# A decoder layer on one core: one ones-product for the FFN norm's squares, and one transpose for both halves of the FFN convolution's columns

## The chip, the core and the metric

The kernel runs on one core of one Trainium2 chip. The core has five engines that run side by side, each with its own queue of instructions: PE (TensorE, matrix products into the PSUM banks), ACT (ScalarE), DVE (VectorE), POOL (GpSimd) and SP, which here only issues DMAs. They wait for each other on counting semaphores. The metric is the device time of one execution in microseconds (us); lower is better.

## The reference

One inference step of a hybrid decoder layer on 512 prompt tokens and 8 x 8 sample tokens, which share all weights. Attention and mLSTM heads give `h`; the change touches only what follows `h`:

```python
def causal_dwconv(x, buf, w):
    width, s = w.shape[0], x.shape[1]
    xx = jnp.concatenate([buf.astype(x.dtype), x], axis=1)
    y = xx[:, :s] * w[0]
    for j in range(1, width):
        y = y + xx[:, j:j + s] * w[j]
    return y, xx[:, s:]
...
    h = x + jnp.concatenate([o_m, o_nsa], axis=-1) @ w_out
    up, f_new = causal_dwconv(rmsnorm(h, g_ffn) @ w_up, f_buf, w_fconv)
    a, g = jnp.split(up, 2, axis=-1)
    y = h + (jax.nn.silu(g) * a) @ w_down
```

`rmsnorm` divides each token by the root of the mean of its 1024 squares. `w_up` is 1024 x 5632 (two halves of 2816, `a` and `g`), `w_down` 2816 x 1024. The convolution has three taps per column; its state holds two rows per sample, and the last two up-projected rows of the prompt and of each sample are outputs (`fconv_p`, `fconv_s`).

## The kernel before

Everything is kept transposed: features on the 128 partitions, the T = 576 tokens along the row. D = 1024 is 8 tiles (KD), the FFN half 2816 is 22 tiles (NFF). Each float32 operand is split into a high and a low part (`hi`, `lo`), and a product is three matmuls (hi x hi, hi x lo, lo x hi), each in two pieces of 256 and 320 columns (UA, UB). The order of each engine's work is written out by hand, with semaphores between the engines.

**Output projection and norm.** `out_tile(m)` (L1582, L1583) makes tile m of `h` in PE; the first three tiles run interleaved. DVE adds `x` (L2377, L2378, semaphore `h_done`), ACT writes the high part `xhi` (L895) and the square `sq` (L898, semaphore `norm_sq`, two buffers in turn), DVE writes the low part `xlo` (L2384). The sum of squares over the 1024 features crosses the partitions, so PE multiplies each tile of squares by a matrix of ones: `square_sum_pe` (L547, L548) accumulates in PSUM banks 6 and 7 over the eight tiles. Two such products stand behind tile 3, two behind tile 4, one behind each of tiles 5, 6 and 7, and the last inside the first up tile. ACT may overwrite a square only when its product is done (`norm_summed`). Then ACT takes the root (L900, L901, semaphore `root`) and DVE the reciprocal (L2387), by which the up projection's results are scaled.

**Up projection.** `up_pe` (L1628, L1630) runs 22 times; the middle 20 are a loop of five trips of four. Each makes one tile of 128 columns of both halves (`w` = 0 and 1), eight steps `k` each. In step k = 7 of the first half (of the second in the first tile) it transposes the convolution's state and taps for these columns: `fin` (16 state rows and 3 tap rows, read by DMA) for each half apart (L1621), into bank 6, from where DVE copies them (L2404). DVE scales the result into a padded tile (L2414 to L2419) and copies the last rows of both halves to `l18` (L2425, L2428). ACT and DVE do the convolution (L908, L2435, L2437), SiLU (L911) and the product (L2441, L2442). Behind the next up tile, PE transposes `l18`, again for each half apart (`last_cols`, L1638), DVE copies the result to `fo` (L2446), and POOL stores it (L537, L538). Every second tile a weight slab is split by ACT (L888) and DVE (L2368); the first slab's split stands ahead of row tile 6 in both queues.

**Down projection.** `down_pe` (L1669, L1670; the last tile L1701) runs 8 times over the 22 tiles of the product. In the first one, step q waits until DVE has written the low part of product tile q (`act_lo`, L2469), and `last_cols(21)` stands ahead of step 12. Output tiles are transposed by L1678.

Of the kernel before, what the change touches and what calls it, by code (L numbers as in the profile page):

```python
# [7 lines left out]
ALU = mybir.AluOpType  # L8
# [47 lines left out]
def hybrid_decoder_layer(nc, A, O):  # L56
    ctx = ExitStack()
    with ctx:
# [299 lines left out]
        def _(pool):  # L358
# [175 lines left out]
            for q in range(NFF):  # L534
                pool.wait_ge(S("u_fo"), q + 2)
                cols = slice(q * P, (q + 1) * P)
                pool.dma_start(O["fconv_p"][0, 0].rearrange("j (w n) -> j w n", w=2)[:, :, cols], fo[0:2]).then_inc(S("u_fos"), 16)  # L537
                pool.dma_start(O["fconv_s"][0].rearrange("b j (w n) -> (b j) w n", w=2)[:, :, cols], fo[2:18])\  # L538
                    .then_inc(S("u_fos"), 16)
                pool.wait_ge(S("u_fos"), 32 * (q + 1))  # L540
                pool.sem_inc(S("u_fof"), 1)


        def square_sum_pe(pe, n, k):

# [447 lines left out]
        def _(pe):  # L993
# [608 lines left out]
            def up_pe(slot, sub, par, qn, norm=False):  # L1602

                hi = whi[slot].rearrange("p (w k n) -> p w k n", w=2, k=KD)
                lo = ring_r[:, slot, :].rearrange("p (w k n) -> p w k n", w=2, k=KD)
                pe.wait_ge(S("u_pad"), qn + 1)
                for w in range(2):
                    for k in range(KD):
                        if norm and w == 0:
                            pe.wait_ge(S("xn_lo"), k + 1)  # L1610
                        if norm and w == 0 and k == 4:
                            square_sum_pe(pe, 2, KD - 1)
                        if norm and w == 1 and k == 0:
                            pe.wait_ge(S("h_done"), KD)
                        if w == norm and k == 6:
                            pe.wait_ge(S("u_fc"), qn + 1)
                        if norm and w == 1 and k == 7:
                            pe.wait_ge(S("root"), MH + 2)
                        if w == norm and k == 7:
                            for z in range(2):  # L1620
                                last = t.transpose(ps[6][:, 32 * z:32 * z + 19], fin[slot][:, z, sub * P:(sub + 1) * P],  # L1621
                                                   ident[0:19, 0:19])
                            last.then_inc(S("u_ft"), 1)
                        c = slice(sub * P, (sub + 1) * P)
                        for n, (wk, x) in enumerate(((hi, xhi[:, k, :]), (hi, xlo[k]), (lo, xhi[:, k, :]))):
                            on = dict(start=(k == 0 and n == 0), stop=(k == KD - 1 and n == 2))
                            first = dict(start=(k == 0 and n == 0 and w == 0), stop=(k == KD - 1 and n == 2))
                            t.matmul(ps[4 + par][:, w * UA:(w + 1) * UA], wk[:, w, k, c], x[:, 0:UA],  # L1628
                                     skip_group_check=True, **first)
                            last = t.matmul(ps[2 * par + w][:, 0:UB], wk[:, w, k, c], x[:, UA:T], **on)  # L1630
                last.then_inc(S("u_mm"), 1)

            def last_cols(qn):

                pe.wait_ge(S("u_l18"), qn + 1)
                pe.wait_ge(S("u_fo"), qn + 1)
                for w in range(2):
                    last = t.transpose(ps[7][0:18, w * P:(w + 1) * P], l18[:, w, :], ident[:])  # L1638
                last.then_inc(S("u_lT"), 1)
# [4 lines left out]
            with pe.Fori(0, 5) as it:  # L1644
                for q in range(4):
                    if q % 2:
                        pe.wait_ge(S("u_lo"), it * 4 + (q + 3))
                    up_pe((q + 1) // 2 % 2, (q + 1) % 2, (q + 1) % 2, it * 4 + (q + 1))
                    last_cols(it * 4 + q)
            up_pe(0, 1, 1, 21)  # L1650
            last_cols(20)

            def down_pe(s, mn, seen, first=False):
# [5 lines left out]
                for q in range(NFF):  # L1659
# [51 lines left out]
        def _(dve):  # L1711
# [658 lines left out]

            for m in range(KD):
# [7 lines left out]
                if m == 0:  # L2379
# [5 lines left out]
                                       in1=xhi[:, m, :].bitcast(F32), op0=ALU.mult, op1=ALU.subtract).then_inc(S("xn_lo"), 1)  # L2385
            dve.wait_ge(S("root"), MH + 2)
# [7 lines left out]
            def up_dve(par, qn, split, before_conv=lambda: None):  # L2394
# [9 lines left out]
                v.tensor_copy(fcol[:, par, :, :], ps[6][:, 0:64].rearrange("p (w n) -> p w n", w=2)[:, :, 0:19]).then_inc(S("u_fc"), 1)  # L2404
# [41 lines left out]
                v.tensor_copy(a7["fo"][0:18, :], ps[7][0:18, 0:256]).then_inc(S("u_fo"), 1)  # L2446
# [98 lines left out]
        def _(sp):  # L2545
# [129 lines left out]
            f_st = A["state_ffn_conv"][0].rearrange("b j (w n) -> (b j) w n", w=2)  # L2675
            f_wt = A["w_fconv"][0].rearrange("j (w n) -> j w n", w=2)

            def up_slab(n):
# [5 lines left out]
                sp.dma_start(fin[s][0:16], f_st[:, :, n * 256:(n + 1) * 256]).then_inc(S(f"slab_in{s}"), 16)  # L2684
                sp.dma_start(fin[s][16:19], f_wt[:, :, n * 256:(n + 1) * 256]).then_inc(S(f"slab_in{s}"), 16)
# [64 lines left out]
```

## Time and profile before

| | us |
|---|---|
| median of three runs (1064.64 to 1066.98) | 1066.34 |
| profiled execution | 1067.79 |
| its span in the trace | 1066.0 |
| PE busy in it | 1016.7 |
| DVE, ACT, POOL busy | 613.3, 404.2, 151.9 |

The profile records each instruction of one execution. 1.8 us of the profiled execution lie outside the span. A group's rows give how long instructions take; where matmuls follow each other without a gap, what one costs is the distance between starts, not its duration, because they overlap. The norm stands at about 574 to 618 us, the up projection at 612.7 to 909, the down projection behind it.

### The profile page before, as it was taken

How to read it: one execution, taken by the hardware profiler on the slowest of the kernel's cores; microseconds unless marked ns; L12 is line 12 of the kernel's file. 1: busy time of each engine (PE TensorE's matmuls, PEld its weight loads, DVE VectorE, ACT ScalarE, POOL GpSimd, SP SyncE). 2: the span in 40 equal slices, each digit the busy share in tenths (PEclk: the TensorE clock that was granted, in tenths of full speed). 3: DMA queues.
4: the chain of work that ended last, by engine and by line, in shares of the span. 5: the costliest groups of instructions: out<-in, count | busy, mean ns of one | idle time of the engine just before them, and what ended most of it. 6: DMA issues, size and time to landing. Idle time of an engine off the chain costs nothing.

```text
span 1066.0 us, 19274 instructions
## 1 busy us (share of the span) xinstructions
PE 1016.7 (95%) x7776; PEld 917.2 (86%) x7776; DVE 613.3 (58%) x1307; ACT 404.2 (38%) x759; POOL 151.9 (14%) x206
## 2 busy tenths in 40 slices
PE   4999999999999979989899999999999999999996
PEld 4999999999867647665469999999999999999996
DVE  3736753444267666678966346676767677932222
ACT  5223422333153455448754233323232323621222
POOL 3200020320112212027730000000000000000000
PEclk9999999999998999989999999999999999999998
DMA  6561162653611266253023022222222222332322
GB/s 186 187 182 40 49 205 64 247 194 122 242 44 42 62 241 239 85 147 105 1 98 113 27 81 82 82 82 82 82 82 82 82 82 56 104 82 72 90 54 89
DMA packets 82076, 114.29 MB, mean 107 GB/s; under 512 B 10086, under 2 KB 72648, under 8 KB 79263
## 3 DMA queue, kind: packets, MB, share of 16 engines
q1 hardware_dynamic: 75247, 70.60, 21.5%
q0 software_dynamic: 6768, 42.84, 10.9%
q8 instruction: 43, 0.70, 0.3%
q14 instruction: 18, 0.15, 0.0%
HBM read 103.33 MB, written 13.59 MB: 110 GB/s over the span
## 4 chain that ended last, share of the span: by engine, by line
PE 85%; DVE 8%; ACT 2%; issue 2%; DMA 1%; POOL 1%; SPq 0%; DVEq 0%; ACTq 0%
PE banks L1630 14%; PE banks L1628 12%; PE banks L1670 6%; PE banks L1129 6%; PE banks L1076 5%; PE banks L1669 5%; PE banks L1079 4%; PE banks L1080 4%; PE banks L1583 3%; PE banks L1113 3%; PE banks L1582 2%; PE banks L1701 2%; PE banks L1404 1%; PE banks L1340 1%; PE banks L1329 1%
## 5 line engine op out<-in xcount | busy, mean ns | idle before, releaser
L1630 PE MATMUL banks<-xnT_r,RB_r 128*128 128x320 f32 x352 | 109.7, 312 | 0.0
L1630 PE MATMUL banks<-xnT_r,ring_r 128*128 128x320 f32 x352 | 109.4, 311 | 0.0
L1628 PE MATMUL banks<-xnT_r,RB_r 128*128 128x256 f32 x352 | 103.2, 293 | 0.0
L1628 PE MATMUL banks<-xnT_r,ring_r 128*128 128x256 f32 x352 | 98.8, 281 | 0.0
L1630 PE MATMUL banks<-RC_r,RB_r 128*128 128x320 f32 x264 | 82.3, 312 | 0.0
L1628 PE MATMUL banks<-RC_r,RB_r 128*128 128x256 f32 x264 | 74.2, 281 | 0.0
L1129 PE MATMUL banks<-RA,RB 128*128 128x128 f32 (+1 forms) x512 | 71.0, 280 | 2.5 <-ACT RA L668 2.5
L2368 DVE TENSOR_TENSOR ring_r<-ring,RB_r 128x2048 fp32r<-128x2048 f32 x22 | 49.4, 2288 | 38.1 <-ACT RB_r L888 38.1
L1628 PEld LDWEIGHTS banks<-xnT_r,RB_r 128*128 128x128 f32 x352 | 67.0, 190 | 1.2
L1129 PEld LDWEIGHTS banks<-RA,RB 128*128 128x128 f32 x512 | 64.1, 188 | 4.0 <-ACT RA L668 3.9
L1628 PEld LDWEIGHTS banks<-xnT_r,ring_r 128*128 128x128 f32 x352 | 67.4, 192 | 0.0
L1630 PEld LDWEIGHTS banks<-xnT_r,RB_r 128*128 128x128 f32 x352 | 66.2, 188 | 0.1
L1630 PEld LDWEIGHTS banks<-xnT_r,ring_r 128*128 128x128 f32 x352 | 66.2, 188 | 0.0
L908 ACT ACTIVATE RA<-RA 128x592 f32<-128x592 f32 x44 | 32.4, 783 | 88.1 <-DVE RA L2419 88.0
L537 POOL DMA_DIRECT2D out_fconv_p_dram<-RA x22 | 12.0, 546 | 356.1 <-DVE RA L2446 341.1
L1076 PE MATMUL banks<-ring_r,xnT_r 128*128 128x256 f32 x200 | 56.1, 280 | 0.0
L1628 PEld LDWEIGHTS banks<-RC_r,RB_r 128*128 128x128 f32 x264 | 50.5, 191 | 0.0
L1630 PEld LDWEIGHTS banks<-RC_r,RB_r 128*128 128x128 f32 x264 | 49.6, 188 | 0.0
L1963 DVE COPY RA<-banks 128x512 f32<-128x512 f32 x32 | 22.1, 691 | 45.1 <-PE banks L1113 45.1
L1670 PE MATMUL banks<-RC_r,RB_r 128*128 128x320 f32 x156 | 46.4, 311 | 0.0
L1076 PE MATMUL banks<-RB_r,xnT_r 128*128 128x256 f32 x160 | 45.1, 282 | 0.0
L1076 PE MATMUL banks<-RB_r,xT_r 128*128 128x256 f32 x160 | 44.8, 280 | 0.0
(656 smaller groups left out, 2927.9 us busy)
## 6 DMA issues: line engine op xcount, KB each, us to landing
ring<-in_w_up_dram SPq DMA_DIRECT2D x22, 1024.0 KB
ring<-in_w_down_dram SPq DMA_DIRECT2D x8, 1408.0 KB, 6.9
ring<-in_w_in_dram SPq DMA_DIRECT2D x10, 1024.0 KB, 6.2
RB<-in_state_win_dram SPq DMA_DIRECT2D x8, 512.0 KB, 5.4
out_win_s_dram<-in_state_win_dram POOLq DMA_DIRECT2D x1, 4032.0 KB
xsp<-RC SPq DMA_DIRECT2D x1, 2304.0 KB, 7.7
xT<-xsp SPq DMA_DIRECT2D x1, 2304.0 KB, 13.7
RA<-in_x_prompt_dram SPq DMA_DIRECT2D x4, 512.0 KB, 5.5
```

Source lines behind the costliest of these rows:

```text
L908: a.activation(c, pad[:, par, w, 0:FVW], ACT.Copy, scale=fcol[:, par, w, 16:17]).then_inc(S("u_tap"), 1)
L1076: last = t.matmul(bank[:, 0:256], x[:, at:at + P], w, **on)
L1079: t.matmul(bank[:, 0:TA], c, x[:, 0:TA], **on)
L1080: last = t.matmul(smp[:, 0:TB], c, x[:, TA:T], **on)
L1113: last = t.transpose(ps[f][:, at:at + P], ct[:, h, j:j + 2, :], ident[:])
L1129: last = t.matmul(ps[4 + kvi][:, 0:w], w1c[:, kvi, half * 8 + 2 * f + c2, :], x, start=(f == 0 and c2 == 0 and half == 0), stop=(f == 3 an ...
L1583: last = t.matmul(ps[2 * (m % 3) + 1][:, 0:UB], w, x[:, UA:T], **on)
L1628: t.matmul(ps[4 + par][:, w * UA:(w + 1) * UA], wk[:, w, k, c], x[:, 0:UA], skip_group_check=True, **first)
L1630: last = t.matmul(ps[2 * par + w][:, 0:UB], wk[:, w, k, c], x[:, UA:T], **on)
L1669: t.matmul(ps[2 * s][:, 0:UA], w, x[:, 0:UA], **on)
L1670: last = t.matmul(ps[2 * s + 1][:, 0:UB], w, x[:, UA:T], **on)
L2368: v.tensor_tensor(ring_r[:, slot, 2048 * w:2048 * (w + 1)], half, whi[slot][:, 2048 * w:2048 * (w + 1)].bitcast(F32), ALU.subtract).then_i ...
```

## The change

Two independent edits in the same stage.

1. **Squares.** ACT writes the first square to a new buffer `sqsum`, and the others to `sq` as before. DVE adds each of the seven others to `sqsum` (`add_squares`), one row tile behind its other work, the last two behind row tile 7. PE then does one product with ones (two matmuls), which has moved to the start of the second half of the first up tile. Seven of the eight products are gone.
2. **Columns.** The two halves' rows lie interleaved on partitions (`fin` 38 x 256 in place of 19 x 512) and, in `l18` and `fo`, along the row and on 36 partitions. So each pair of transposes is one: L1621's output has 38 columns, L1638's stationary operand 36. DVE's copy to `fo` is 36 x 128 where it was 18 x 256. The DMAs that fill `fin` and empty `fo` move the same bytes in the same number of calls. The waits for `u_l18` and `u_fo`, ahead of `last_cols`, stand one step (k = 7) earlier.

```diff
-        fin = [z[0:19, :, :].rearrange("p a b -> p (a b)").rearrange("p (w n) -> p w n", w=2) for z in (kcT_s, vc_s)]
+        fin = [z[0:38, :, :].rearrange("p a b -> p (a b)")[:, 0:256] for z in (kcT_s, vc_s)]
...
-        l18 = a7["l18"].rearrange("p (w n) -> p w n", w=2)
-        fo = a7["fo"][0:18, :].rearrange("p (w n) -> p w n", w=2)
+        l18 = a7["l18"].rearrange("p (n w) -> p w n", w=2)
+        fo = a7["fo"][0:36, 0:P]
...
-        def square_sum_pe(pe, n, k):
+        def square_sum_pe(pe):
 
-            pe.wait_ge(S("norm_sq"), KD * (n - 2) + k + 1)
-            nc.tensor.matmul(ps[6][:, 0:TA], ones[:], sq[:, k % 2, 0:TA], start=(k == 0), stop=(k == KD - 1))
-            nc.tensor.matmul(ps[7][:, 0:TB], ones[:], sq[:, k % 2, TA:T], start=(k == 0),
-                             stop=(k == KD - 1)).then_inc(S("norm_summed"), 1)
+            pe.wait_ge(S("norm_summed"), KD - 1)
+            nc.tensor.matmul(ps[6][:, 0:TA], ones[:], sqsum[:, 0:TA], start=True, stop=True)
+            nc.tensor.matmul(ps[7][:, 0:TB], ones[:], sqsum[:, TA:T], start=True, stop=True).then_inc(S("norm_summed"), 1)
...
-                if k >= 2:
-                    act.wait_ge(S("norm_summed"), k - 1)
-                a.activation(sq[:, k % 2, :], xT[:, k, :], ACT.Square).then_inc(S("norm_sq"), 1)
+                if k >= 3:
+                    act.wait_ge(S("norm_summed"), k - 2)
+                a.activation(sq[:, k % 2, :] if k else sqsum, xT[:, k, :], ACT.Square).then_inc(S("norm_sq"), 1)
...
                 out_tile(m, 0, KD)
-                for k in {3: (0, 1), 4: (2, 3)}.get(m, (m - 1,)):
-                    square_sum_pe(pe, 2, k)
...
-                        if norm and w == 0 and k == 4:
-                            square_sum_pe(pe, 2, KD - 1)
                         if norm and w == 1 and k == 0:
                             pe.wait_ge(S("h_done"), KD)
+                            square_sum_pe(pe)
...
+                        if cols is not None and w == 1 and k == 7:
+                            pe.wait_ge(S("u_l18"), cols + 1)
+                            pe.wait_ge(S("u_fo"), cols + 1)
...
                         if w == norm and k == 7:
-                            for z in range(2):
-                                last = t.transpose(ps[6][:, 32 * z:32 * z + 19], fin[slot][:, z, sub * P:(sub + 1) * P],
-                                                   ident[0:19, 0:19])
-                            last.then_inc(S("u_ft"), 1)
+                            t.transpose(ps[6][:, 0:38], fin[slot][:, sub * P:(sub + 1) * P], ident[0:38, 0:38])\
+                                .then_inc(S("u_ft"), 1)
...
             def last_cols(qn):
 
-                pe.wait_ge(S("u_l18"), qn + 1)
-                pe.wait_ge(S("u_fo"), qn + 1)
-                for w in range(2):
-                    last = t.transpose(ps[7][0:18, w * P:(w + 1) * P], l18[:, w, :], ident[:])
-                last.then_inc(S("u_lT"), 1)
+                t.transpose(ps[7][0:36, 0:P], a7["l18"], ident[:]).then_inc(S("u_lT"), 1)
...
+            def add_squares(n):
+
+                dve.wait_ge(S("norm_sq"), n + 1)
+                if n > 1:
+                    dve.wait_ge(S("norm_summed"), n - 1)
+                v.tensor_tensor(sqsum, sqsum, sq[:, n % 2, :], ALU.add).then_inc(S("norm_summed"), 1)
...
+                if m >= 2:
+                    add_squares(m - 1)
+            add_squares(KD - 1)
...
-                v.tensor_copy(fcol[:, par, :, :], ps[6][:, 0:64].rearrange("p (w n) -> p w n", w=2)[:, :, 0:19]).then_inc(S("u_fc"), 1)
+                v.tensor_copy(fcol[:, par, :, :], ps[6][:, 0:38].rearrange("p (n w) -> p w n", w=2)).then_inc(S("u_fc"), 1)
...
-                v.tensor_copy(a7["fo"][0:18, :], ps[7][0:18, 0:256]).then_inc(S("u_fo"), 1)
+                v.tensor_copy(fo, ps[7][0:36, 0:P]).then_inc(S("u_fo"), 1)
```

In the lists below a row is a line of the code, an operation, output <- inputs and the output's shape, and in brackets the semaphores that it waits for; lines of the changed code have other numbers. First PE's queue between row tile 7 of the output projection and the first up tile, before:

```order
L1582 MATMUL banks<-RC_r,ring_r 128x256
L1583 MATMUL banks<-RC_r,ring_r 128x320
L547 MATMUL banks<-RC,ones 128x288 [waits norm_sq]
L548 MATMUL banks<-RC,ones 128x288
L1628 MATMUL banks<-xnT_r,RB_r 128x256 [waits u_pad,xn_lo,u_lo,h_done]
```

The same place now, and the only ones-product left, between the halves of the first up tile:

```order
L1581 MATMUL banks<-RC_r,ring_r 128x256
L1582 MATMUL banks<-RC_r,ring_r 128x320
L1625 MATMUL banks<-xnT_r,RB_r 128x256 [waits u_pad,xn_lo,u_lo,h_done]
L1627 MATMUL banks<-xnT_r,RB_r 128x320
...
L547 MATMUL banks<-RC,ones 128x288 [waits norm_summed,h_done]
L548 MATMUL banks<-RC,ones 128x288
L1625 MATMUL banks<-xnT_r,RB_r 128x256
```

The product is no longer in front of the up tile, and the one that is left waits for DVE's sums (`norm_summed`) and not for ACT's square. Next DVE's queue from row tile 5 to the reciprocal, before:

```order
L2384 SCALAR_TENSOR_TENSOR RC_r<-xT,vcol,xnT_r 128x576 [waits xn_hi,h_done]
L2368 TENSOR_TENSOR ring_r<-ring,RB_r 128x2048 [waits u_hi] x2
L2377 TENSOR_TENSOR xT<-xT,banks 128x256 [waits h_mm]
L2378 TENSOR_TENSOR xT<-xT,banks 128x320
...
L2387 RECIPROCAL RA<-RC 128x576 [waits root]
```

And now:

```order
L2386 SCALAR_TENSOR_TENSOR RC_r<-xT,vcol,xnT_r 128x576 [waits xn_hi,h_done]
L2371 TENSOR_TENSOR RC<-RC 128x576 [waits norm_summed,norm_sq]
L2363 TENSOR_TENSOR ring_r<-ring,RB_r 128x2048 [waits u_hi] x2
L2379 TENSOR_TENSOR xT<-xT,banks 128x256 [waits h_mm]
L2380 TENSOR_TENSOR xT<-xT,banks 128x320
...
L2371 TENSOR_TENSOR RC<-RC 128x576 [waits norm_summed,norm_sq] x2
L2392 RECIPROCAL RA<-RC 128x576 [waits root]
```

An add of squares (L2371) stands behind each low part from row tile 2 on, ahead of the slab's split, and two behind the last. Last, PE's queue at the end of an up tile in the loop, before:

```order
L1628 MATMUL banks<-xnT_r,ring_r 128x256
L1630 MATMUL banks<-xnT_r,ring_r 128x320
L1638 MATMUL banks<-ident,RA 18x128 [waits u_fo,u_l18]
L1638 MATMUL banks<-ident,RA 18x128
L1628 MATMUL banks<-xnT_r,RB_r 128x256 [waits u_pad]
```

And now:

```order
L1625 MATMUL banks<-xnT_r,RB_r 128x256 [waits u_fo,u_l18]
L1627 MATMUL banks<-xnT_r,RB_r 128x320
L1625 MATMUL banks<-RC_r,RB_r 128x256
L1627 MATMUL banks<-RC_r,RB_r 128x320
L1625 MATMUL banks<-xnT_r,ring_r 128x256
L1627 MATMUL banks<-xnT_r,ring_r 128x320
L1632 MATMUL banks<-ident,RA 36x128
L1625 MATMUL banks<-xnT_r,RB_r 128x256 [waits u_pad]
```

One transpose of 36 rows stands where two of 18 stood, and its two waits have moved six matmuls up.

## Rows read from the trace of the kernel before

**Rows 1.** Page, section 1: busy us, share, instructions.
```profile
PE 1016.7 (95%) x7776; PEld 917.2 (86%) x7776; DVE 613.3 (58%) x1307; ACT 404.2 (38%) x759; POOL 151.9 (14%) x206
```

**Rows 2.** Windows: busy us (count) by engine, granted clock, DMA share, GB/s.
```profile
574.00:895.00 321.00, 321.00 (x2367) 314.11 (x2366) 197.95 (x386) 112.93 (x117) 20.10 (x38) 1.00 0.25 79
895.00:929.00 34.00, 32.35 (x243) 31.71 (x241) 32.59 (x60) 17.77 (x28) 3.16 (x6) 1.00 0.21 61
929.00:1056.00 127.00, 127.00 (x961) 126.99 (x961) 34.53 (x51) 28.44 (x93) 0.00 (x0) 1.00 0.27 75
```

**Rows 3.** Timeline, PE: start, us, engine, line, operation, tiles, shape.
```profile
611.76 0.31 PE L1583 MATMUL banks<-RC_r,ring_r 128*128 128x320 f32 x1
611.91 0.65 PE L547 MATMUL banks<-RC,ones 128*128 128x288 f32 x2
...
613.00 0.31 PE L1630 MATMUL banks<-xnT_r,RB_r 128*128 128x320 f32 x1
```

**Rows 4.** Timeline, PE and weight loads, at one L1621.
```profile
632.52 0.31 PE L1630 MATMUL banks<-xnT_r,ring_r 128*128 128x320 f32 x1
632.76 0.29 PE L1621 MATMUL banks<-ident,kvc 19*128 19x19 f32 x2
...
633.20 0.31 PE L1630 MATMUL banks<-xnT_r,RB_r 128*128 128x320 f32 x1
...
632.75 0.20 PEld L1621 LDWEIGHTS banks<-ident,kvc 19*128 19x128 f32 x2 [0.16 <-issue]
```

**Rows 5.** Timeline, PE, at two L1638.
```profile
640.13 0.31 PE L1630 MATMUL banks<-xnT_r,ring_r 128*128 128x320 f32 x1
640.28 0.38 PE L1638 MATMUL banks<-ident,RA 128*18 128x128 f32 x2
...
640.61 0.31 PE L1630 MATMUL banks<-xnT_r,RB_r 128*128 128x320 f32 x1
...
653.71 0.38 PE L1638 MATMUL banks<-ident,RA 128*18 128x128 f32 x2
```

**Rows 6.** Groups by line and shape, PE: busy us, mean ns, idle.
```profile
L1638 PE MATMUL banks<-ident,RA 128*18 128x128 f32 x44 | 8.4, 271 | 0.0
...
L1621 PE MATMUL banks<-ident,kvc 19*128 19x19 f32 x44 | 6.5, 223 | 0.0
```

**Rows 7.** Timeline, DVE, row tile 6 to the first up tile.
```profile
601.40 4.49 DVE L2368 TENSOR_TENSOR ring_r<-ring,RB_r 128x2048 fp32r<-128x2048 f32 x2 [1.49 <-ACT RB_r L888]
...
613.84 0.82 DVE L2384 SCALAR_TENSOR_TENSOR RC_r<-xT,vcol,xnT_r 128x576 fp32r<-128x576 f32 x1 [0.92 <-ACT xnT_r L895]
...
626.28 0.20 DVE L2404 COPY RA<-banks 128x38 f32<-128x38 f32 x1 [4.16 <-PE banks L1621]
```

**Rows 8.** Timeline, ACT, the first slab's split.
```profile
599.47 3.70 ACT L888 ACTIVATE RB_r<-ring 128x2048 fp32r<-128x2048 f32 x2
```

**Rows 9.** Window behind the first slab's issue, columns as in group 2.
```profile
592.00:598.00 6.00, 6.00 (x45) 5.84 (x44) 0.64 (x2) 0.00 (x0) 0.00 (x0) 1.00 0.00 0
```

**Rows 10.** Timeline, DVE, passage from up to down.
```profile
895.99 0.41 DVE L2446 COPY RA<-banks 18x256 f32<-18x256 f32 x1 [5.00 <-PE banks L1638]
...
924.52 0.41 DVE L2446 COPY RA<-banks 18x256 f32<-18x256 f32 x1
```

**Rows 11.** Timeline, PE, the same passage.
```profile
925.65 0.39 PE L1669 MATMUL banks<-RB_r 128*128 128x256 f32 x1 [1.65 <-DVE RC_r L2469]
```

**Rows 12.** Lines on DVE: ns min/median/max, first and last start.
```profile
L2469 DVE TENSOR_TENSOR RC_r<-RC,RC_r x8: 746/747/751, 901.6 to 918.4; 128x576 fp32r<-128x576 f32 x8
...
L2446 DVE COPY RA<-banks x22: 405/406/413, 642.2 to 924.5; 18x256 f32<-18x256 f32 x22
...
L2404 DVE COPY RA<-banks x22: 174/175/200, 626.3 to 910.1; 128x38 f32<-128x38 f32 x22
```

**Rows 13.** Waits of PE's weight loads: us, times, longest.
```profile
PEld banks L1329 <- issue: 14.6, 18, 0.8
...
PEld banks L1621 <- issue: 3.6, 22, 0.2
```

More of the change, by code:

```diff
@@ L243, in hybrid_decoder_layer @@
         ca, cg = a7["ca"], a7["cg"]
-        fin = [z[0:19, :, :].rearrange("p a b -> p (a b)").rearrange("p (w n) -> p w n", w=2) for z in (kcT_s, vc_s)]
+        fin = [z[0:38, :, :].rearrange("p a b -> p (a b)")[:, 0:256] for z in (kcT_s, vc_s)]
         fcol = a7["fcol"].rearrange("p (s w n) -> p s w n", s=2, w=2)
-        l18 = a7["l18"].rearrange("p (w n) -> p w n", w=2)
-        fo = a7["fo"][0:18, :].rearrange("p (w n) -> p w n", w=2)
+        l18 = a7["l18"].rearrange("p (n w) -> p w n", w=2)
+        fo = a7["fo"][0:36, 0:P]
         rstd_h = a7["rstd"]
-        an = carve(c["kv"], [("sq", 2 * T), ("rms", T), ("rstd", T)])
+        an = carve(c["kv"], [("sq", 2 * T), ("rms", T), ("rstd", T), ("sqsum", T)])
         sq = an["sq"].rearrange("p (s t) -> p s t", s=2)
-        rms, rstd = an["rms"], an["rstd"]
+        rms, rstd, sqsum = an["rms"], an["rstd"], an["sqsum"]
         actT = RC[:, 0:NFF * T].rearrange("p (k t) -> p k t", k=NFF)
@@ L536, in _ @@
                 cols = slice(q * P, (q + 1) * P)
-                pool.dma_start(O["fconv_p"][0, 0].rearrange("j (w n) -> j w n", w=2)[:, :, cols], fo[0:2]).then_inc(S("u_fos"), 16)
-                pool.dma_start(O["fconv_s"][0].rearrange("b j (w n) -> (b j) w n", w=2)[:, :, cols], fo[2:18])\
+                pool.dma_start(O["fconv_p"][0, 0].rearrange("j (w n) -> (j w) n", w=2)[:, cols], fo[0:4]).then_inc(S("u_fos"), 16)
+                pool.dma_start(O["fconv_s"][0].rearrange("b j (w n) -> (b j w) n", w=2)[:, cols], fo[4:36])\
                     .then_inc(S("u_fos"), 16)
@@ L1597, in _, with up_pe @@
                 out_tile(m, 0, KD)
-                for k in {3: (0, 1), 4: (2, 3)}.get(m, (m - 1,)):
-                    square_sum_pe(pe, 2, k)
             pe.wait_ge(S("h_done"), KD - 1)
-            def up_pe(slot, sub, par, qn, norm=False):
+            def up_pe(slot, sub, par, qn, norm=False, cols=None):
                 hi = whi[slot].rearrange("p (w k n) -> p w k n", w=2, k=KD)
@@ L1647, in _ @@
                         pe.wait_ge(S("u_lo"), it * 4 + (q + 3))
-                    up_pe((q + 1) // 2 % 2, (q + 1) % 2, (q + 1) % 2, it * 4 + (q + 1))
+                    up_pe((q + 1) // 2 % 2, (q + 1) % 2, (q + 1) % 2, it * 4 + (q + 1), cols=it * 4 + q)
                     last_cols(it * 4 + q)
-            up_pe(0, 1, 1, 21)
+            up_pe(0, 1, 1, 21, cols=20)
             last_cols(20)
@@ L1665, in down_pe @@
                         if q == 12:
+                            pe.wait_ge(S("u_l18"), NFF)
+                            pe.wait_ge(S("u_fo"), NFF)
                             last_cols(21)
@@ L2674, in _ @@
             w_dn = A["w_down"][0].rearrange("(k p) n -> p k n", p=P)
-            f_st = A["state_ffn_conv"][0].rearrange("b j (w n) -> (b j) w n", w=2)
-            f_wt = A["w_fconv"][0].rearrange("j (w n) -> j w n", w=2)
+            f_st = A["state_ffn_conv"][0].rearrange("b j (w n) -> (b j w) n", w=2)
+            f_wt = A["w_fconv"][0].rearrange("j (w n) -> (j w) n", w=2)
             def up_slab(n):
@@ L2683, in up_slab @@
                     sp.dma_start(dst[:, w], w_up[:, w, :, n * 256:(n + 1) * 256]).then_inc(S(f"slab_in{s}"), 16)
-                sp.dma_start(fin[s][0:16], f_st[:, :, n * 256:(n + 1) * 256]).then_inc(S(f"slab_in{s}"), 16)
-                sp.dma_start(fin[s][16:19], f_wt[:, :, n * 256:(n + 1) * 256]).then_inc(S(f"slab_in{s}"), 16)
+                sp.dma_start(fin[s][0:32], f_st[:, n * 256:(n + 1) * 256]).then_inc(S(f"slab_in{s}"), 16)
+                sp.dma_start(fin[s][32:38], f_wt[:, n * 256:(n + 1) * 256]).then_inc(S(f"slab_in{s}"), 16)
             sp.wait_ge(S("o_dve"), 1)
```

## The prediction

> **What bounds the kernel now.** I read first the page's busy times: PE is busy 95% of the span, DVE 58% [rows 1]. Such an average does not say what an edit in one stage is worth, so I then took the windows of the stage that is edited. From 574 to 895 PE is busy 321.00 of 321 us at the full granted clock, DVE 197.95; from 929 to 1056 PE is busy 127.00 of 127. Between them is the only hole: 895 to 929 has 32.35 of 34, and there DVE is busy 32.59 [rows 2]. So up to 895 what leaves PE's queue is gained one for one, unless PE must then wait. In the hole something else sets the time. The timeline shows one wait of PE, 1.65 us until 925.65, for DVE's L2469 [rows 11], and DVE had itself last waited at 895.99, for 5.00 us, for PE's L1638 [rows 10]. The path goes from PE to DVE at 895.99 and back to PE at 925.65; between them only what DVE does counts.
>
> **The squares on PE.** Where matmuls overlap, I cost by the distance between starts. An up tile's period in the loop is 653.71 - 640.28 = 13.43 us [rows 5]; less the two places with transposes (0.41 and 0.21, below) that is 12.81 for 48 pairs of matmuls, 0.267 a pair. L1583 at 611.76 and L1630 at 613.00, with one product (L547, L548) between them, are 1.24 apart [rows 3], so one product costs 0.97 us. Eight become one: 7 x 0.97 = **6.8 us**. All eight stand in the stretch where PE never idles.
>
> **Does PE wait for DVE's sums instead?** The product that is left waits for seven adds. Each is a 128 x 576 float32 operation on SBUF, the shape of L2469, which takes 0.747 [rows 12]. With a wait of 0.92 ahead of each, as DVE has for ACT ahead of L2384 [rows 7], it would be 1.7, the upper bound; none would wait for ACT if the square is always done first, 0.75, which I take, since the adds stand one row tile behind. The tight part is the end, so I made a timetable of it. Four of the removed products stood ahead of the end of row tile 5, five ahead of tile 6's, six ahead of tile 7's. Tile 5 thus ends 3.9 us earlier. ACT's split of the first slab follows it, so it moves from 599.47 [rows 8] to 595.6. The slab must be there by then: no DMA moves anything after 592 [rows 9], so it is, with 3.6 us of room. DVE's split (601.40 to 605.89 [rows 7]) then ends at about 602.0. Row tile 6's own work takes DVE and ACT 2.6 us more, as tile 7's does (612.07, where L1583 ends [rows 3], to 614.66 [rows 7]), add 5 another 0.75: 605.3. PE ends tile 7 at 612.07 - 5.8 = 606.3; DVE's part of it ends at 608.9, and adds 6 and 7 at 610.4. PE needs the sum after tile 7 and one half of an up tile, 24 x 0.267 = 6.4 us: at 612.7. That is 2.3 us of room, and 0.4 even at 1.7 for each of the last two adds. I take no wait, 0.
>
> **The root and the reciprocal.** The product now stands four steps of 0.8 = 3.2 us later in its tile. Before, DVE idled 4.16 us between the reciprocal and its first copy L2404 [rows 7]; about 0.9 is left as cover. Were it gone, DVE would run late by the excess, and PE would notice only at the third up tile, which reuses the first one's banks, 13 us on. 0.
>
> **The transposes of the state (L1621).** From 632.52 to 633.20 is 0.68 us, against 0.267 for a pair: the place costs 0.41. Two transposes last 0.29 together [rows 4] and one 0.223 alone [rows 6], so the second adds 0.07. The rest is idle time where the shape changes: 0.16 ahead of the weight load [rows 4], and as much again behind. One transpose of 38 columns keeps those. From below: nothing is saved, if the wider one lasts as long as two. From above: half the place, 0.205. I take 0.07, since these rows separate the parts. 21 such places stand before 895: 21 x 0.07 = **1.4 us** (0 to 4.3).
>
> The Trainium skill has a rule for this place: TensorEngine Tiling (Array Packing), section Key Properties, says that a change of the tiling mode drains TensorE. By it, 19 rows and 38 rows both mean a change away from the full array and one back, so that the drain stays and 1.4 us it is; the idle 0.16 in the row agrees. Applied to the 18 and then 36 stationary columns of L1638 it would mean such a drain there too; the rows of the next part show none, and there the measurement decides.
>
> **The transposes of the last rows (L1638).** From 640.13 to 640.61 is 0.48 us, less 0.267 is 0.21 for two. Two last 0.38 [rows 5], one 0.271 [rows 6]: 0.11 each and no idle time. One goes at each of 20 places before 895.6: 20 x 0.107 = **2.1 us** (1.0, if the one that is left has a start-up of its own, to 2.2). The two waits that moved six matmuls up are for `fo` of the tile before, copied 0.4 us after its transpose (L1638's end of a tile, at 895.6, to 895.99 [rows 10]) where the next wait comes 12.6 later, and for `l18`, which DVE writes right behind the tile's results, ahead of all its convolution work. 0.
>
> **The passage to the down projection.** Here PE's savings, one L1621 and two L1638, together 0.28, only become idle time, and DVE's count. L2404 copies 38 elements a partition in 0.175, L2446 256 in 0.406 [rows 12]: 0.00106 each, so the copy of 128, on 36 partitions, takes 0.27 and saves 0.135. Three of these lie on the path (the two of [rows 10] and one between): **0.4 us** (0 to 0.5). PE's wait becomes 1.65 + 0.28 - 0.40 = 1.5.
>
> **DMAs.** `fin` and `fo` keep their bytes, in rows of 1 KB and 512 B, in as many calls; POOL, busy 14% [rows 1], has an up tile's time for each store. 0.
>
> **Sum.** 6.8 + 1.4 + 2.1 + 0.4 = 10.7; unrounded 10.8. Against the profiled execution, 1067.79 (its span 1066.0 and 1.8 outside), that gives 1057.0. That execution lies 1.45 above the median of the runs, so for the median I forecast 1066.34 - 10.8 = **1055.5**.
>
> **Rivals.** (a) *The transposes cost in proportion.* If the idle time at L1621 belongs to each transpose and not to the change of shape, half the place goes: 0.135 more at 21 places, 2.9 us, 1052.6. Against it stand 0.29 for two and 0.223 for one. Chance 0.07.
> (b) *The sum comes late*, and PE waits between the halves of the first up tile. The price is one for one beyond 2.3 us of room. Adds 5 to 7 hang on the slab's split; if that starts 3.9 us later than in my timetable, at its old place, PE waits 1.6, and with 0.95 for each of two late adds on top 3.5: 1057.1 to 1059. Against it, the slab has landed and ACT has nothing else ahead. Chance 0.08.
> (c) *Slower*: a wait takes the place of the second transpose. PE's weight loads stood idle 0.8 us at a time ahead of L1329, 14.6 us in 18 times, for nothing that the profile shows; ahead of L1621 it was 3.6 us in 22 [rows 13]. If the 38-row transpose met the longer gap, each place would cost 0.64 more than I count, 13.4 in all: 1055.5 + 13.4 = 1068.9. It decides from a gap of 0.16 + 10.8 / 21 = 0.67. For it, 38 rows is a shape that the loop has not had; against it, the gap at L1621 is the same 0.16 all 22 times, so it goes with the change of shape and not with its size. Chance 0.03.
> (d) *The change does not reach the end*: the hole takes the gain back, because the path there does not begin with PE. Then only 0.4 stays, 1065.9. Against it, the 5.00 us that DVE had waited at 895.99 [rows 10]. Chance 0.02.
>
> **How the numbers follow.** 0.80 for the forecast, with a range of its own of 1054.2 to 1057 (its unknown costs, and about 1 us for how medians spread). The range 1052.6 to 1059.0 adds (a) and (b). A measurement of this kernel can tell 0.2%, some 2 us, from no change. Faster by more than that: the forecast, (a) and (b), 0.95, less a little for what I did not see, 0.94. Within 0.2%: 0.03. Slower: 0.03.
>
> **What would show it.** In the changed kernel's profile: two matmul records on L547 and two on L548, where there were 16 each; PE busy without a gap at the product near 612.7, and the last add of squares done some 2 us ahead of it; the reciprocal at about 615, some 3 us earlier, and about 0.9 us of idle DVE before the first copy of columns; an up tile's period of 13.26 in place of 13.43; the copy to `fo` at 0.27; one wait of PE of about 1.5 us in the passage, for the same DVE operation; PE full behind it. I am wrong if PE idles between the halves of the first up tile, if the period falls by 0.3 or not at all, or if the granted clock is not full there.

## The result and the profile after

| | before | after |
|---|---|---|
| median, measured together (us) | 1066.66 (1064.64 to 1068.37) | 1055.48 (1054.79 to 1056.37) |
| ratio | | 0.9902, 95% interval 0.9885 to 0.9919 |
| profiled execution | 1067.79 | 1056.03 |
| its span | 1066.0 | 1054.3 |
| PE busy | 1016.7 | 1004.5 |
| DVE, ACT, POOL busy | 613.3, 404.2, 151.9 | 615.4, 403.9, 151.6 |

The forecast was 1055.5. The changed kernel is 1.0% faster. Lines have other numbers in it: the ones-product is still L547 and L548, the adds of squares are L2371, the up matmuls L1625 and L1627, the state's transpose L1619, that of the last rows L1632, their copies L2409 and L2451, `act_lo` L2474, the down matmuls L1664 and L1665.

First the windows of the edited stages, of the changed kernel (columns as in [rows 2]). They answer to [rows 2], with the place of the product taken out by itself:

```profile
574.00:608.00 34.00, 34.00 (x258) 34.00 (x257) 19.41 (x30) 13.07 (x16) 0.00 (x0) 1.00 0.24 78
608.00:620.00 12.00, 12.00 (x88) 11.58 (x87) 6.08 (x10) 0.90 (x2) 0.00 (x0) 1.00 0.42 140
620.00:884.00 264.00, 264.00 (x1952) 259.13 (x1951) 174.10 (x356) 98.25 (x97) 19.76 (x38) 1.00 0.25 80
884.00:918.00 34.00, 32.46 (x242) 31.86 (x241) 32.98 (x62) 18.01 (x29) 3.11 (x6) 1.00 0.22 61
918.00:1044.00 126.00, 126.00 (x954) 125.99 (x953) 33.76 (x50) 27.89 (x91) 0.00 (x0) 1.00 0.27 75
```

PE is still full everywhere but in the passage, at the full granted clock. So each microsecond that left its queue has left the span.

PE's timeline at the product that is left answers to [rows 3]:

```profile
611.19 0.31 PE L1627 MATMUL banks<-xnT_r,ring_r 128*128 128x320 f32 x1
611.34 0.65 PE L547 MATMUL banks<-RC,ones 128*128 128x288 f32 x2
611.82 0.65 PE L548 MATMUL banks<-RC,ones 128*128 128x288 f32 x2
612.09 0.50 PE L1625 MATMUL banks<-xnT_r,RB_r 128*128 128x256 f32 x1
612.43 0.31 PE L1627 MATMUL banks<-xnT_r,RB_r 128*128 128x320 f32 x1
```

No brackets stand behind L547: PE did not wait. From 611.19 to 612.43 it is again 1.24 for a pair and a product. DVE's timeline up to it answers to [rows 7]:

```profile
594.80 0.75 DVE L2371 TENSOR_TENSOR RC<-RC 128x576 f32<-128x576 f32 x1
596.37 4.49 DVE L2363 TENSOR_TENSOR ring_r<-ring,RB_r 128x2048 fp32r<-128x2048 f32 x2 [0.82 <-ACT RB_r L887]
...
603.25 0.75 DVE L2371 TENSOR_TENSOR RC<-RC 128x576 f32<-128x576 f32 x1
605.13 0.42 DVE L2379 TENSOR_TENSOR xT<-xT,banks 128x256 f32<-128x256 f32 x1 [1.14 <-PE banks L1582]
...
607.61 1.61 DVE L2371 TENSOR_TENSOR RC<-RC 128x576 f32<-128x576 f32 x2
613.43 3.75 DVE L2392 RECIPROCAL RA<-RC 128x576 f32<-128x576 f32 x1 [4.21 <-ACT RC L900]
...
618.28 0.20 DVE L2409 COPY RA<-banks 128x38 f32<-128x38 f32 x1 [0.92 <-PE banks L1619]
```

The adds wait for nobody. The last two end at 609.2, 2.1 us ahead of the product, and behind the reciprocal 0.92 us of idle DVE are left, where there were 4.16.

PE's timeline at one transpose of the state, with the weight loads, answers to [rows 4]; the two transposes of last rows, 19 tiles apart, answer to [rows 5]:

```profile
617.76 0.31 PE L1627 MATMUL banks<-xnT_r,ring_r 128*128 128x320 f32 x1
618.00 0.25 PE L1619 MATMUL banks<-ident,kvc 38*128 38x38 f32 x1
618.18 0.38 PE L1625 MATMUL banks<-xnT_r,RB_r 128*128 128x256 f32 x1
618.40 0.31 PE L1627 MATMUL banks<-xnT_r,RB_r 128*128 128x320 f32 x1
```

```profile
618.00 0.14 PEld L1619 LDWEIGHTS banks<-ident,kvc 38*128 38x128 f32 x1 [0.16 <-issue]
618.18 0.19 PEld L1625 LDWEIGHTS banks<-xnT_r,RB_r 128*128 128x128 f32 x1
```

```profile
632.23 0.27 PE L1632 MATMUL banks<-ident,RA 128*36 128x128 f32 x1
...
884.30 0.27 PE L1632 MATMUL banks<-ident,RA 128*36 128x128 f32 x1
```

The place of L1619 takes 0.64 - 0.267 = 0.37 us in this instance. The period of an up tile is (884.30 - 632.23) / 19 = 13.27, where before it was 13.44, (895.57 - 640.28) / 19 with the start of L1638 at the end of the last tile.

Last the passage, DVE's copy and PE's wait, which answer to [rows 10] and [rows 11]:

```profile
884.60 0.28 DVE L2451 COPY RA<-banks 36x128 f32<-36x128 f32 x1 [4.92 <-PE banks L1632]
```

```profile
913.88 0.39 PE L1664 MATMUL banks<-RB_r 128*128 128x256 f32 x1 [1.54 <-DVE RC_r L2474]
```

From DVE's copy to PE's resumption it was 925.65 - 895.99 = 29.66 us, and is 913.88 - 884.60 = 29.28.

**Where the time went.** The two profiled executions differ by 11.8 us, more than the sum. To leave out what lies ahead of the change, I took in every trace the distance from the first L1583 (L1582) of the output projection to the last matmul of the down projection, the **stretch** below. It runs from 555.24 to 1056.11 before, 500.9 us, and from 554.07 to 1044.34 after, 490.3: 10.6 us. The other 1.2 us had been gained before the first changed instruction. Over the nine traces of this study that start lies between 553.3 and 555.7, so it is the spread of executions. The stretch itself repeats well: the period of an up tile is 13.437 in before and in e1, which have the same loop, and 13.267 in the changed kernel, e2, e5 and e7, which share theirs.

### The profile page after: what moved, and what is told of

Same layout as the page of the kernel before. It is cut to its first block, busy times and chain, and to the rows that moved or that the text cites. A ratio compares the mean times of both kernels' runs of the same rounds, so it can differ in the third digit from the quotient of the medians.

```text
span 1054.3 us, 19143 instructions
## 1 busy us (share of the span) xinstructions
PE 1004.5 (95%) x7704; PEld 906.4 (86%) x7704; DVE 615.4 (58%) x1314; ACT 403.9 (38%) x759; POOL 151.6 (14%) x206
## 4 chain that ended last, share of the span: by engine, by line
PE 85%; DVE 8%; ACT 2%; issue 2%; DMA 1%; POOL 1%; SPq 0%; DVEq 0%; ACTq 0%
PE banks L1627 14%; PE banks L1625 12%; PE banks L1665 6%; PE banks L1128 6%; PE banks L1075 5%; PE banks L1664 5%; PE banks L1078 4%; PE banks L1079 4%; PE banks L1582 3%; PE banks L1112 3%; PE banks L1581 2%; PE banks L1696 2%; PE banks L1403 1%; PE banks L1339 1%; PE banks L1328 1%
## 5 line engine op out<-in xcount | busy, mean ns | idle before, releaser
L1627 PE MATMUL banks<-xnT_r,RB_r 128*128 128x320 f32 x352 | 109.6, 311 | 0.0
L1627 PE MATMUL banks<-xnT_r,ring_r 128*128 128x320 f32 x352 | 109.3, 311 | 0.0
L1625 PE MATMUL banks<-xnT_r,RB_r 128*128 128x256 f32 x352 | 103.1, 293 | 0.0
L1625 PE MATMUL banks<-xnT_r,ring_r 128*128 128x256 f32 x352 | 98.8, 281 | 0.0
L1627 PE MATMUL banks<-RC_r,RB_r 128*128 128x320 f32 x264 | 82.3, 312 | 0.0
L1625 PE MATMUL banks<-RC_r,RB_r 128*128 128x256 f32 x264 | 74.2, 281 | 0.0
L1625 PEld LDWEIGHTS banks<-xnT_r,RB_r 128*128 128x128 f32 x352 | 67.0, 190 | 1.8
L1625 PEld LDWEIGHTS banks<-xnT_r,ring_r 128*128 128x128 f32 x352 | 67.4, 192 | 0.0
L1627 PEld LDWEIGHTS banks<-xnT_r,RB_r 128*128 128x128 f32 x352 | 66.2, 188 | 0.1
L1627 PEld LDWEIGHTS banks<-xnT_r,ring_r 128*128 128x128 f32 x352 | 66.1, 188 | 0.0
L1625 PEld LDWEIGHTS banks<-RC_r,RB_r 128*128 128x128 f32 x264 | 50.6, 192 | 0.0
L1627 PEld LDWEIGHTS banks<-RC_r,RB_r 128*128 128x128 f32 x264 | 49.6, 188 | 0.0
L1665 PE MATMUL banks<-RC_r,RB_r 128*128 128x320 f32 x156 | 46.4, 312 | 0.0
```

The source lines that it names most:

```text
L1665: last = t.matmul(ps[2 * s + 1][:, 0:UB], w, x[:, UA:T], **on)
```

## The experiments

Each kernel is compared by its median with the kernel before, run beside it (1067.04 for e1, e2, e3 and e5; 1065.55 for e4, e6 and e7; 1066.66 for the changed kernel, as above), and by its stretch in the trace.

| kernel | median | ratio (95%) | stretch | against |
|---|---|---|---|---|
| before | 1067.04, 1065.55 | | 500.9 | |
| after | 1055.48 | 0.9902 (0.9885 to 0.9919) | 490.3 | before: 10.6 less |
| e1, squares only | 1058.66 | 0.9921 (0.9903 to 0.9940) | 494.1 | before: 6.8 less |
| e2, columns only | 1061.89 | 0.9958 (0.9940 to 0.9976) | 497.1 | before: 3.8 less |
| e3, state in 128 rows | 1051.35 | 0.9855 (0.9836 to 0.9875) | 484.8 | after: 5.5 less |
| e4, transpose twice | 1056.15 | 0.9901 (0.9880 to 0.9923) | 491.7 | after: 1.4 more |
| e5, product at k = 1 | 1061.45 | 0.9945 (0.9930 to 0.9961) | 496.6 | after: 6.4 more |
| e7, product at k = 4 | 1056.31 | 0.9914 (0.9898 to 0.9930) | 491.6 | after: 1.3 more |
| e6, e3 and three `act_lo` on POOL | 1053.24 | 0.9873 (0.9851 to 0.9894) | 486.2 | e3: 1.4 more |

### One edit at a time: e1 and e2

e1 is the kernel before with the first edit alone (`add_squares`, `sqsum` and the one product, as in the diff of the change), e2 with the second alone (`fin`, `l18`, `fo`, the two transposes and their copies).

> The kernel before with the first edit alone: DVE adds the squares, PE has one ones-product; all transposes as before. The prediction's sum: 6.8 us less than before (ratio 0.9936, 1059.8 us by the runs of before at 1066.66), no wait of PE between the halves of the first up tile, an up tile's period still 13.43 to 13.44, PE's wait in the passage 1.65. Rival (the gain of the whole change is mostly from the columns, or products overlap with something): less than 5 us.

> The kernel before with the second edit alone: one transpose where two stood, ones-products as before. Sum of the prediction: 1.4 + 2.1 + 0.4 = 3.9 us less than before (ratio 0.9963). The trace of the changed kernel, where one L1621 place became 0.045 us cheaper and one L1638 place 0.104, gives 0.9 + 2.1 + 0.4 = 3.4; its tile period fell by 0.17 and not by 0.15, which would give 3.8. Rival: parts of the two edits are worth more together than apart, then both this run and the squares alone fall short, and their gains add to clearly less than 11.

The squares gave 6.8 us in the stretch and the columns 3.8, together 10.6 where both edits give 10.6. So they don't touch each other, and neither hides the other's gain. PE's wait in the passage was 1.6 in e1 and 1.5 in e2. That the squares' gain is 6.8 without the other edit rules out that the columns' edit paid for a part of it.

### Is the idle time at the state's transpose one of a change of shape? e3

The forecast took the idle time at L1621 for a cost of the change from full rows to few and back, not of the transposes. If so, a transpose of all 128 rows should have none of it, though it multiplies more.

```diff
+        fin_all = [z.rearrange("p a b -> p (a b)")[:, 0:256] for z in (kcT_s, vc_s)]
...
-                            t.transpose(ps[6][:, 0:38], fin[slot][:, sub * P:(sub + 1) * P], ident[0:38, 0:38])\
+                            t.transpose(ps[6][:, 0:P], fin_all[slot][:, sub * P:(sub + 1) * P], ident[:])\
```

> The changed kernel, but the transpose of the state reads all 128 rows (90 of them are left over from earlier work and end in columns that nobody reads) and gives 128 x 128. If the idle 0.16 us on each side of the 38-row transpose comes from the change of the array's shape, it goes: the place costs 0.11 as the 128-row transpose of the last rows does, not 0.38, at 21 places before the passage, 5.6 us less: 1049.9 us, ratio to before 0.985. Rival: the idle time comes from the transpose as such, or from where its data lie (a tile that a DMA filled); then the time stays at 1055.5, or rises by some 0.06 us a place for the wider output, 1056.7.

PE's timeline of e3 at the same place (L1620 is the transpose, L1628 the second matmul of a pair), and its weight loads:

```profile
618.34 0.31 PE L1628 MATMUL banks<-xnT_r,ring_r 128*128 128x320 f32 x1
618.50 0.27 PE L1620 MATMUL banks<-ident,kvc 128*128 128x128 f32 x1
618.52 0.36 PE L1626 MATMUL banks<-xnT_r,RB_r 128*128 128x256 f32 x1
618.72 0.31 PE L1628 MATMUL banks<-xnT_r,RB_r 128*128 128x320 f32 x1
```

```profile
618.23 0.19 PEld L1628 LDWEIGHTS banks<-xnT_r,ring_r 128*128 128x128 f32 x1
618.36 0.14 PEld L1620 LDWEIGHTS banks<-ident,kvc 128*128 128x128 f32 x1
618.50 0.19 PEld L1626 LDWEIGHTS banks<-xnT_r,RB_r 128*128 128x128 f32 x1
```

The transpose lasts longer (0.27 for 0.25), and the place costs less: 618.72 - 618.34 - 0.267 = 0.11 for 0.37. The weight load of 128 rows starts at 618.36, while the matmul ahead still runs; in the changed kernel that of 38 rows started at 618.00, after 0.16 of idle time. Behind it the next full load started at 618.18, after 0.05 of idle time and not "as much again", as the forecast had it; the rest of the cost there lies in the starts, since the full matmul behind a 38-row transpose starts 0.18 after it and the one behind a 128-row transpose 0.02. Over all 22 places the mean is 0.116 here and 0.378 in the changed kernel: 0.26 x 21 = 5.5 us, and the stretch is 5.5 shorter. The wait in the passage grew to 1.8, since PE now comes earlier to a point that DVE sets. So two thirds of the place go with the change of row count and back. The tile that is read is the same, which rules out the rival that the gap comes from where the data lie. The Trainium skill's sentence on this (TensorEngine Tiling (Array Packing), Key Properties: a change of tiling mode drains TensorE) agrees with the trace for rows: it gives no figure, and here avoiding the change there and back is worth 0.26 us.

e3 is the fastest kernel of this study: its interval ends at 0.9875, where that of the changed kernel begins at 0.9885.

### What one more transpose costs behind the first: e4

The forecast's 0.07 for the second transpose came from durations. e4 issues each 38-row transpose twice, which measures it as a distance.

```diff
+                            t.transpose(ps[6][:, 0:38], fin[slot][:, sub * P:(sub + 1) * P], ident[0:38, 0:38])
                             t.transpose(ps[6][:, 0:38], fin[slot][:, sub * P:(sub + 1) * P], ident[0:38, 0:38])\
```

> The changed kernel with each 38-row transpose of the state issued twice, to the same place. If the drain belongs to the change of shape, as the run with full rows says, a second transpose of the same shape costs only its own 0.07 to 0.09: 21 x 0.08 = 1.7 us more than the changed kernel in the trace, 1057.2. Rival (a) of the prediction, that the idle time belongs to each transpose: 0.38 more at 21 places, 8 us, 1063.5.

PE's timeline of e4 at the place:

```profile
618.72 0.31 PE L1628 MATMUL banks<-xnT_r,ring_r 128*128 128x320 f32 x1
618.96 0.25 PE L1619 MATMUL banks<-ident,kvc 38*128 38x38 f32 x1
619.04 0.23 PE L1620 MATMUL banks<-ident,kvc 38*128 38x38 f32 x1
619.20 0.39 PE L1626 MATMUL banks<-xnT_r,RB_r 128*128 128x256 f32 x1
619.42 0.31 PE L1628 MATMUL banks<-xnT_r,RB_r 128*128 128x320 f32 x1
```

The place costs 619.42 - 618.72 - 0.267 = 0.43; the mean over 22 is 0.440, against 0.378 with one. So a second transpose of the same shape adds 0.062, and 21 of them 1.3 us; the stretch grew by 1.4. That is near the forecast's 0.07, and not rival (a), by which a second one would have cost as much as the first. It also closes a gap that e3 left: e3 changed the moving columns too, from 38 to 128. Here the second transpose has 38 columns like the first and starts 0.08 behind it; the delay comes only where the rows change back, 0.16 to the full matmul at 619.20. A single 38-row transpose of 0.378 is thus 0.062 for itself and 0.316 for the change of rows; in e3 the change is gone and the transpose itself costs 0.116. The medians (1056.15 and 1055.48, each beside its own runs of before) agree but could not have shown it alone.

### Where the room of the product ends: e5 and e7

The forecast's timetable gave the product 2.3 us of room; the trace of the changed kernel shows 2.1. Moving the product ahead of where it stands tells where the room ends, and whether beyond it each microsecond earlier costs one microsecond of waiting. e7 puts it at step 4 of the first half (3.2 us earlier), e5 at step 1 (5.6 us earlier):

```diff
+                        if norm and w == 0 and k == 4:
+                            square_sum_pe(pe)
...
-                            square_sum_pe(pe)
```

(e5 the same with `k == 1`.)

> The changed kernel with the one ones-product at step 1 of the first half of the first up tile, not between its halves. In the changed kernel's trace the last add of squares ended at 609.2, the first up tile began at 604.9 and its step 1 comes at 605.7. Theory (the room is what the timetable says, and beyond it the price is one for one): PE waits 3.5 us there, 1059.0 us in all, ratio to before 0.9935. Rival: the wait is absorbed, because PE's time in the up stage is handed back in the passage where DVE sets the end; then 1055.5. A second rival: the idle stretch lets the granted clock fall to its lower level, and more than 3.5 is lost.

> The changed kernel with the ones-product at step 4 of the first half, where the last of the eight stood before. PE comes there at 608.1 and the last add ends at 609.2 in the changed kernel's trace: a wait of 1.1 us. If the 6.5 us that the earlier place (step 1) cost were 3.5 of wait and 3 of lower clock, and a short wait does not bring the clock down, as the 1.5 us in the passage does not, this costs 1.1: 1056.6. Rival: any wait there brings the clock down, and it costs some 4 us: 1059.6.

PE's timeline of e7, then of e5, at the product:

```profile
609.43 0.31 PE L1628 MATMUL banks<-xnT_r,ring_r 128*128 128x320 f32 x1
610.81 0.72 PE L547 MATMUL banks<-RC,ones 128*128 128x288 f32 x2 [1.07 <-DVE RC L2372]
```

```profile
608.93 1.30 PE L547 MATMUL banks<-RC,ones 128*128 128x288 f32 x2 [3.46 <-DVE RC L2372]
610.03 1.17 PE L548 MATMUL banks<-RC,ones 128*128 128x288 f32 x2
```

In e7 PE waits 1.07, which is 3.2 - 2.1, for the add of squares (L2372 there), and the stretch grows by 1.3. The wait is shorter than the delay, because matmuls overlap: the product starts 610.81 - 609.43 = 1.38 behind the matmul ahead, where without a wait it was 611.34 - 611.19 = 0.15, so it is 1.23 late. So rival (b)'s price was right, one for one beyond the room. In e5 the wait is 3.46, close to 5.6 - 2.1, but the stretch grows by 6.4. The windows of e5 show the other 2.9 us (the column with 1.00, 0.96 and 0.50 is the granted clock):

```profile
604.00:606.00 2.00, 1.47 (x11) 1.23 (x10) 0.82 (x2) 0.44 (x1) 0.00 (x0) 1.00 0.07 10
606.00:608.00 2.00, 0.00 (x0) 0.00 (x0) 1.49 (x2) 0.91 (x2) 0.00 (x0) 0.96 0.93 300
608.00:610.00 2.00, 1.07 (x2) 0.84 (x3) 0.76 (x1) 0.00 (x0) 0.00 (x0) 0.50 1.09 364
610.00:612.00 2.00, 2.00 (x8) 1.69 (x7) 0.00 (x0) 0.77 (x2) 0.00 (x0) 0.50 1.10 349
612.00:614.00 2.00, 2.00 (x10) 2.00 (x10) 1.84 (x1) 0.12 (x1) 0.00 (x0) 0.50 0.15 46
614.00:616.00 2.00, 2.00 (x15) 2.00 (x14) 1.93 (x3) 0.00 (x0) 0.00 (x0) 0.84 0.00 0
616.00:618.00 2.00, 2.00 (x17) 2.00 (x17) 0.09 (x2) 0.00 (x0) 0.00 (x0) 1.00 0.00 0
```

PE idled from 605.5, the granted clock fell near 607.8 to 0.50, the lower of its two levels (1.2 GHz), and it stayed there until about 614.7, though PE was busy again from 608.93. In a window at that level PE got through 10 matmuls, at the full one through 17. 5.7 us at half the pace are a loss of 2.9. After e7's wait of 1.07 the clock was 1.00 all through, as after the 1.54 of the passage. My sum for e5's first theory, of the wait alone, was therefore too small, and the theory with the clock was right.

### Can POOL take DVE's work in the passage? e6

With e3, PE waits 1.8 us in the passage for DVE. e6 is e3 with three of DVE's subtractions (`act_lo`, n = 15 to 17) on POOL, which has little to do there.

```diff
+                if q == NFF - 2:
+                    for n in (15, 16, 17):
+                        k = FIRST[n]
+                        pool.wait_ge(S("a_hi"), n + 1)
+                        g.tensor_tensor(alo[k], actT[:, k, :], ahi[k].bitcast(F32), ALU.subtract).then_inc(S("a_lp"), 1)
...
-            up_dve(1, 21, lambda: [act_lo(n) for n in range(EARLY, 18)])
+            up_dve(1, 21, lambda: [act_lo(n) for n in range(EARLY, 15)])
```

> The kernel with full rows, and three of the twelve low parts that DVE computes in a row in the passage from up to down (its operations of 0.67 each) go to POOL, which takes 1.40 for this shape. Theory (in the passage only what DVE does counts): DVE's path is 2.0 us shorter and PE's wait, 1.8 us there, goes: 1.8 us less than the kernel with full rows, 1049.5, PE busy 34 of 34 us in the window of the passage. Rival: POOL is too late for steps 15 to 17 of the first down tile, or slows DVE through the memory that they share, and PE waits there instead: no gain or a loss of up to 1.5 us.

It got slower by 1.4 us in the stretch. The intervals of e3's and e6's ratios overlap, so that rests on the two traces. The waits of PE's L1673 (down) in e6, in 884 to 925 (us in total, times, longest); L547 is here the line of POOL's subtraction:

```profile
PE banks L1673 <- DVE RC_r L2483: 2.2, 1, 2.2
...
PE banks L1673 <- POOL RC_r L547: 0.8, 1, 0.8
```

Why DVE was late with less to do is in the timelines of e6, of POOL (with the ns min/median/max of its last two) and then of DVE:

```profile
901.66 2.63 POOL L547 TENSOR_TENSOR RC_r<-RC,RC_r 128x576 fp32r<-128x576 f32 x1 [5.70 <-ACT RC_r L935]
904.25 3.86 POOL L547 TENSOR_TENSOR RC_r<-RC,RB_r 128x576 fp32r<-128x576 f32 x2
```

```profile
L547 POOL TENSOR_TENSOR RC_r<-RC,RB_r x2: 1947/1949/1951, 904.2 to 906.2; 128x576 fp32r<-128x576 f32 x2
```

```profile
901.57 1.42 DVE L2483 TENSOR_TENSOR RC_r<-RC,RC_r 128x576 fp32r<-128x576 f32 x2
902.91 2.00 DVE L2449 SCALAR_TENSOR_TENSOR RA<-RA 128x592 f32<-128x592 f32 x1
904.95 1.89 DVE L2451 SCALAR_TENSOR_TENSOR RA<-RA 128x592 f32<-128x592 f32 x1
906.76 1.98 DVE L2449 SCALAR_TENSOR_TENSOR RA<-RA 128x592 f32<-128x592 f32 x1
908.78 0.84 DVE L2451 SCALAR_TENSOR_TENSOR RA<-RA 128x592 f32<-128x592 f32 x1
```

In e3 each of these two lines takes 0.83 or 0.84, all 44 times. In e6 the three that run while POOL subtracts (901.66 to 908.1) take 2.00, 1.89 and 1.98, and the fourth, behind it, 0.84. That is 3.4 us more, against three subtractions that stand 0.67 apart, 2.0 saved: DVE is 1.4 late, and that is what the stretch lost too. The Trainium skill bears on this: GPSIMD Engine Reference, section 1. Specifications, has POOL's interfaces to SBUF shared with VectorE's, with contention for DVE instructions of two SBUF inputs, which these are. The trace agrees, with 0.83 going to 2.0.

The ends show how the two share: they take turns. POOL's three end at 904.29, 906.20 and 908.11, and DVE's three at 904.91, 906.84 and 908.74, each 0.62 to 0.64 behind POOL's. POOL's in turn end some 1.3 behind the DVE operation ahead of each (902.99, 904.91, 906.84). By this reading DVE's last two subtractions, L2483, had POOL's first waiting: they kept their 0.75 each, and it took 2.63 where the next two took 1.95. POOL's L476 has the same shape of output and takes 1.40 in the trace of before, the value that the forecast of e6 used; the waiting on both sides is what it left out. Why POOL came in behind the second of those subtractions and not the first is open, and so is whether that form would ever give way as L2449 and L2451 did.

## Why the prediction was right, step by step

Times of the changed kernel are compared after adding the 1.2 us by which its stage starts earlier in the trace.

- **The squares on PE: right.** 7 x 0.97 = 6.8, and e1 measured 6.8.
- **No wait for the sums: right, and so was the timetable.** An add takes 0.75, the value taken (the bound was 1.7). ACT's split of the slab started at 594.45 (595.6 with the shift; 595.6 forecast), the adds ended at 609.2 (610.4; 610.4 forecast), the product started at 611.34 (612.5; 612.7 forecast). The room is 2.1 for 2.3. e7 showed that it is real: 3.2 us earlier cost 1.07 us of waiting.
- **Root and reciprocal: right.** 613.43 (614.6) for about 615, with 0.92 of cover for 0.9, and nobody was late.
- **The transposes of the last rows: right.** The place went from a mean of 0.216 to 0.113, so 0.103 for 0.107, 2.1 us in 20 places.
- **The transposes of the state: right in kind, the term was too large.** The mechanism, a fixed cost of the change of shape that one transpose pays as two did, is what e3 and e4 show. But the place went from a mean of 0.422 to 0.378, which is 0.044 for 0.07: 0.9 us in 21 places and not 1.4. The step that failed is the size of the second transpose, 0.07, taken from durations (0.29 for two less a mean of 0.223), though matmuls overlap, and the forecast itself costs the squares by distances between starts. To this comes that the wider transpose costs a little more. Two of 38 columns cost 0.440 (e4) and two of 19 cost 0.422, so one wider is 0.009 more if the two share the difference, an estimate. The second of 19 columns was then 0.053, and 0.053 - 0.009 is the 0.044 that was measured. The "as much again behind" is not what the trace shows (0.05 of idle time), but no term of the sum used it.
- **The passage: right.** The copy takes 0.276 (0.27), PE waits 1.54 (1.5), and copy to resumption is 0.38 us shorter (0.40).
- **The sum.** The terms as measured make 6.8 + 0.9 + 2.1 + 0.4 = 10.2. The stretch has 10.6. An up tile's period fell by 0.17, of which the two places explain 0.15; the 0.02 left is 0.4 us in 20 tiles, spread over 48 pairs of matmuls. It comes with the edit of the columns, since e2's period fell by the same 0.17 and e1's not at all; its cause is open. So the forecast's 10.8 is near 10.6 in part by luck: a term that was 0.5 too large stands beside 0.4 that no term had.
- **The rivals.** (a) falls by e4. (b) did not happen, its price holds by e7, and it lacked a part: in e5 a wait of 3.46 us took the clock down as well, so its worst case, a wait of 3.5, would have cost some 3 us more than the 1059 that it was given. (c), a longer gap at the 38-row transpose, did not happen: the gap is 0.16 all 22 times (3.6 us in total, as before). (d) did not happen either; the passage's wait shrank by 0.1 and took nothing back.

What the forecast did not see is that the larger gain lay in the part that it treated as fixed. Of the 0.378 us of a place with one transpose, the change of rows is 0.316; e3 removes it, pays 0.05 more for a transpose of 128 rows, and gains 0.26 a place.

## What to carry to other kernels

On an engine that never idles, cost an edit by distances between starts, not by durations: the squares (6.8 forecast and measured) went by distances, the state's transposes (1.4 for 0.9) by durations. Where the shape changes as well, ask what the new one costs. A small matmul of few rows between full ones costs the change of rows there and back (0.32 us here) on top of itself (0.06). With all 128 rows, if need be with rows that nobody reads, it cost 0.12 in all; merging two small ones saved only 0.04. When work moves off a full PE to an engine with slack, make the timetable of the place where the result is needed: the room (2.1 us here) decides. And a long wait can cost clock too: the one of 3.46 us cost another 2.9.

## What the runs showed of the hardware

- A transpose with 38 rows between matmuls of 128 costs 0.378 us of PE, with 128 rows 0.116, though its record is longer (0.273 for 0.255). A second one of 38 rows right behind adds 0.062. PE's weight loads idle 0.16 ahead of the 38-row one and 0.05 behind it. A stationary operand of 18 or 36 columns over all rows has no such cost: 0.11 a transpose.
- A wait of PE of 3.46 us took the granted clock from 1.00 to 0.50 and kept it there for 5.7 us after PE had resumed, about 2.9 us of loss; waits of 1.07 (e7), 1.54 (after), 1.8 (e3) and 2.2 us (e6) took nothing.
- Operations of DVE and POOL with two float32 inputs in SBUF ended in turns (e6). DVE's `scalar_tensor_tensor` on 128 x 592 takes 0.83 us alone and 1.9 to 2.0 when it starts while POOL subtracts, ending 0.62 to 0.64 behind POOL's. POOL's subtraction of 128 x 576 took 1.95 and 2.63, each some 1.3 behind the end of the DVE operation ahead.
